# Hybrid MLA/GLA layer on one core: the MLA setup reordered on all engines, its last third moved into the first attention head

## The reference, cut to what matters

```python
cq, ckv, kr, gq, gk, gv, gr, gg = split(x @ w_in)         # 384, 256, 64, 256, 256, 512, 16, 512
# A) MLA, 4 heads of 128 + 64
q = (rms_norm(cq, q_norm) @ w_uq).reshape(B, T, 4, 192)
q_rope = apply_rope(q[..., 128:], cos, sin)
k_rope = apply_rope(kr, cos, sin)
ckv = rms_norm(ckv, kv_norm)
s = causal((q_nope . w_uk . ckv) + (q_rope . k_rope)) * MLA_SCALE
mla = softmax(s) @ ckv @ w_uv
# B) GLA, 4 heads, chunks of 64 tokens
loga = log_sigmoid(gr @ w_gate2 + b_gate) / 16
S_t = diag(exp(loga_t)) S_(t-1) + k_t^T v_t;  o_t = q_t S_t
gla = rms_norm(o, gla_norm) * silu(gg)
x = layer_norm(ALPHA * x + concat(mla, gla) @ w_out)
y = layer_norm(ALPHA * x + square(relu(x @ w1)) @ w2)     # 4096 wide
```

## Time and profile before

| what | value |
|---|---|
| median of 3 runs | 1426.96 us (1426.54 to 1427.34) |
| the profiled execution | 1429.95 us |
| its span | 1428.3 us |
| mean granted clock of TensorE | 0.97 |
| PE busy | 1344.7 us, 94% of the span, 8796 instructions |
| PEld busy | 1260.5 us, 88% |
| DVE busy | 605.7 us, 42%, 950 instructions |
| ACT busy | 414.4 us, 29% |
| POOL busy | 158.8 us, 11% |
| DMA | 123.38 MB, mean 86 GB/s |

### The profile page before, as it was taken

One profiled execution on the slowest core, in us unless ns is written; L12 is line 12 of the kernel. 1 busy time (PEld: TensorE's weight loads), 2 busy tenths in 40 slices (PEclk: granted clock), 3 DMA queues, 4 the chain that ended last, 5 costly groups with the idle time before them and its releaser, 6 DMA issues.

```text
span 1428.3 us, 22125 instructions
## 1 busy us (share of the span) xinstructions
PE 1344.7 (94%) x8796; PEld 1260.5 (88%) x8796; DVE 605.7 (42%) x950; ACT 414.4 (29%) x677; POOL 158.8 (11%) x195
## 2 busy tenths in 40 slices
PE   7998999999878897999999999999999999999996
PEld 7986868787657776899999999999999999999996
DVE  4122222445776776565532422314233133242558
ACT  3212332234534445534411302203022031120225
POOL 4424333010000000042000000000000000004022
PEclk9999999999879998999999999999999999999998
DMA  8658886413300011312120301102012020020103
GB/s 285 206 181 266 281 281 217 119 60 95 107 17 10 10 45 60 104 46 59 58 62 1 95 24 59 59 0 88 29 39 79 0 88 29 29 88 0 59 1 119
DMA packets 100593, 123.38 MB, mean 86 GB/s; under 512 B 11123, under 2 KB 84997, under 8 KB 100518
## 3 DMA queue, kind: packets, MB, share of 16 engines
q1 hardware_dynamic: 94374, 105.59, 23.5%
q0 software_dynamic: 6144, 16.79, 3.7%
HBM read 108.42 MB, written 13.93 MB: 86 GB/s over the span
## 4 chain that ended last, share of the span: by engine, by line
PE 80%; SPq 7%; DVE 7%; issue 3%; ACT 2%; DMA 1%; POOL 0%; DVEq 0%; ACTq 0%; POOLq 0%
PE psum L2120 24%; PE psum L2148 22%; PE psum L355 9%; PE psum L1843 6%; PE psum L1353 5%; SPq L267 3%; SPq L270 3%; PE psum L2087 3%; PE psum L1664 2%; PE psum L2081 2%; DVE softmax_stats L1735 1%; PE psum L904 1%; PE psum L901 1%; DVE pT_lo L1753 1%; PE psum L1673 1%
## 5 line engine op out<-in xcount | busy, mean ns | idle before, releaser
L2177 ACT ACTIVATE hid_tmp<-psum 128x1032 f32<-128x1032 f32 x32 | 33.1, 1035 | 531.0 <-PE psum L2120 526.4
L355 PE MATMUL psum<-xTh,win_hi 128*128 128x344 f32 (+1 forms) x432 | 150.5, 348 | 9.7 <-DVE xTl L408 9.7
L2120 PE MATMUL psum<-x_hi,w_hi 128*128 128x344 f32 x720 | 153.2, 321 | 0.0
L2120 PE MATMUL psum<-x_lo,w_hi 128*128 128x344 f32 x720 | 152.8, 320 | 0.0
L2120 PE MATMUL psum<-x_hi,w_lo 128*128 128x344 f32 x720 | 152.0, 319 | 0.0
L2148 PE MATMUL psum<-hid_hi,w_hi 128*128 128x344 f32 x672 | 142.6, 320 | 0.0
L2148 PE MATMUL psum<-hid_lo,w_hi 128*128 128x344 f32 x672 | 142.4, 320 | 0.0
L2148 PE MATMUL psum<-hid_hi,w_lo 128*128 128x344 f32 x672 | 141.8, 319 | 0.0
L355 PE MATMUL psum<-xTl,win_hi 128*128 128x344 f32 (+1 forms) x432 | 141.5, 328 | 0.0
L355 PE MATMUL psum<-xTh,win_lo 128*128 128x344 f32 (+1 forms) x432 | 141.5, 328 | 0.0
L2242 DVE TENSOR_TENSOR z_T<-z_T,psum 128x1032 f32<-128x1032 f32 x48 | 59.0, 1229 | 186.7 <-PE psum L2148 186.7
(11 more groups left out here) (387 smaller groups left out, 2182.1 us busy)
## 6 DMA issues: line engine op xcount, KB each, us to landing
mlp_raw<-in_w SPq DMA_DIRECT2D x64, 512.0 KB, 4.3
k_pages<-in_pages SPq DMA_DIRECT2D x128, 160.0 KB, 3.2
v_pages<-in_pages POOLq DMA_DIRECT2D x128, 128.0 KB, 4.2
win_raw<-in_w_in SPq DMA_DIRECT2D x17, 512.0 KB, 6.6
scratch<-proj_stage SPq DMA_DIRECT2D x13, 516.0 KB, 5.1
x_T_raw<-in_x_T SPq DMA_DIRECT2D x6, 688.0 KB, 9.2
z_T<-in_x_T SPq DMA_DIRECT2D x3, 1376.0 KB, 6.2
out_y_T<-z_T SPq DMA_DIRECT2D x12, 344.0 KB, 2.4
```

The source lines that it names most:

```text
L355: mm = pe.matmul(psum[0:M, 3 * (m % 2) + b, 0:BLK], w[:, m % 2, k, 0:M], x[:, k, b * BLK:(b + 1) * BLK], start=(k == 0 and i == 0), stop=( ...
L2120: mm = pe.matmul(psum[:, 3 * (i % 2) + b, 0:BLK], w[:, i % 2, k], x[:, k, C3[b]], start=(k == 0 and n == 0), stop=(k == KD - 1 and n == 2))
L2177: act.activation(ht[:, i % 2, :].rearrange("p (b c) -> p b c", b=3), mlp_set(i), ACT.Relu).then_inc(h_free, 1)
```

## The change

It touches the order of the work, not its amount: no product is added or left out.

1. **Gate loads.** In `sp_project` the call of `sp_gates_in` moves from ahead of tile 6's work to behind the issue of tile 6's store.
2. **State stores.** The four stores of the sample's GLA state leave `sp_gla` for `sp_gla_sample`, which is called ahead of `sp_heads_in`, so that they stand ahead of the load of cq.
3. **Rotary tables** get buffers of their own (in the room of the even key's high and low part) and are loaded behind the key rows, with no wait for "nk". The second pair gets its own input and temporary (`xr2`, `rtmp2`).
4. **Query sums.** The squares and their additions move up into GLA's slots 46 to 50 (`act_cq_squares`, `dve_cq_sum`), with rows of `mixT` as their place (`sqrow`); "nq" moves to the end of the "gla_bank" ring, behind gT0 to gT3. Head weights and rotary weights are split in slots 46 to 50.
5. **Head 0's query and key blocks** are done within the setup (`QK_FIRST`), right behind pair 0's swaps. "head_bank" now continues the counts of "gla_bank".
6. **Into the first head** (table `EXTRA`, by unit v): pair 1's swaps (0), eight value blocks (2 to 5), gT4 to gT7 and gTs (3 to 5), GLA's second root, normalisation and sample (`dve_gla_normed`, 2); the even key's split and pair 1's low part (1). Head 1's query blocks go from units 2 and 4 to units 5 and 6.

The table and the functions that run it:

```diff
@@ sp_project @@
-                if m == ROW_KR + 1:
-                    sp_gates_in(sp)
...
                 sp.dma_start(scratch[m, 0:rows, :], pstage[0:rows, m % 2, :]).then_inc(proj_stored[m % 2], 16)
+                if m == ROW_KR + 1:
+                    sp_gates_in(sp)
                 after(3 * m + 2)
...
@@ ring of banks 6 and 7 in GLA and setup @@
-                   44: [("sO",)], 47: [("nk",)], 50: [("gT", 0), ("gT", 1)], 53: [("gT", t) for t in range(2, 5)]}
+                   44: [("sO",)], 47: [("nk",)]}
         SLOTS = 12 * (NT - ROW_GG)
-        gb = Banks("gla_bank", [6, 7], [task for s in range(SLOTS + 6) for task in gla_tasks(s)] + [("gT", t) for t in range(5, 8)] + [("gTs",)])
+        GLA_LAST = [("gT", 0), ("gT", 1), ("gT", 2), ("gT", 3), ("nq",)]
...
@@ sp_gla @@
+        def sp_gla_sample(sp):
             sp.wait_ge(st_done, 4)
...
@@ ScalarE, slots 46, 48 and after @@
+        def act_cq_squares(act, k):
+            if k == 0:
+                act.wait_ge(cq_loaded, 16)
+                act.wait_ge(cksq_done, 3)
+            elif k == 1:
+                gb.wait(act, ("nk",))
+            else:
+                act.wait_ge(cqsum_done, 1)
+            act.activation(sqrow[0 if k else 1], cqraw[:, k], ACT.Square).then_inc(cqsq_done, 1)
...
@@ VectorE, slots 49 and after @@
+        def dve_cq_sum(dve, k):
+            dve.wait_ge(cqsq_done, k + 1)
+            dve.tensor_tensor(sqrow[1], sqrow[1], sqrow[0], ALU.add).then_inc(cqsum_done, 1)
...
@@ SyncE, rotary tables @@
-            gb.wait(sp, ("nk",))
-            r = a["rope"].rearrange("p (c t) -> p c t", c=2)
-            for i in range(2):
-                sp.dma_start(rope[i], r[:, i, 0:TP]).then_inc(rope_loaded, 16)
...
+            r = a["rope"].rearrange("p (c t) -> p c t", c=2)
+            for i in range(2):
+                sp.dma_start(rope[i][:], r[:, i, 0:TP]).then_inc(rope_loaded, 16)
...
@@ pe_mla_in @@
-            split(pe, "cq2")
-            pe_rope_in(pe, 0)
-            for t in range(NORM_A, 8):
+            pe_rope_in(pe, 0, 1)
+            for t in (1, 2, 3):
                 pe_gla_task(pe, ("gT", t))
-            pe_gla_task(pe, ("gTs",))
-            pe_rope_swap(pe, 0)
-            pe_rope_in(pe, 1)
-            mb.begin(pe, ("nq",))
-            pe.wait_ge(cqsum_done, 2)
-            mb.full(pe_norm_sums(pe, mb.of(("nq",)), cqsq[:, 0]))
-            pe_rope_swap(pe, 1)
-            split(pe, "uv")
-            for t in range(8):
-                mb.begin(pe, ("v", t))
-                c = slice(t * P, (t + 1) * P)
-                mb.full(passes(pe, mb.of(("v", t)), [((ckh[:, k, c], ckl[:, k, c]), (wuvh[:, k], wuvl[:, k])) for k in range(2)]))
+            pe_gla_task(pe, ("nq",))
+            pe_rope_swap(pe, 0, mb)
+            pe_qk(pe, ("q", 0, 0)), pe_qk(pe, ("q", 0, 1))
+            pe_rope_in(pe, 1, 0)
+            split(pe, "ck1")
+            pe_qk(pe, ("k", 0, 0)), pe_qk(pe, ("k", 0, 1))
+            pe_rope_in(pe, 1, 1)
 
...
@@ dve_mla_in, behind the key's low parts @@
-            lo_of(dve, "kr0")
+            gated(dve, 2)
+            variance(dve, 1)
+            gated(dve, 3)
+            dve_var_rms(dve, 1, ("nq",), 3 * P)
             dve.wait_ge(gst_stored, 80)
-            lo_of(dve, "kr1"), lo_of(dve, "uv")
-            dve_rope(dve, 0)
+            lo_of(dve, "kr1")
+            dve_qk(dve, ("q", 0, 0)), dve_qk(dve, ("q", 0, 1))
+            dve_rope(dve, 0, mb)
-            dve_var_rms(dve, 1, mb, ("nq",), 3 * P)
-            dve_rope(dve, 1)
-            lo_of(dve, "q1")
+            dve_qk(dve, ("k", 0, 0)), dve_qk(dve, ("k", 0, 1))
-            for t in range(8):
-                lo_of(dve, f"v{t}")
-            head_lo(dve, 0)
-
...
@@ the table, and the ring of the heads @@
+        EXTRA = {0: [("qs", 1, 0), ("qs", 1, 1)], 2: [("v", 0), ("v", 1), ("v", 2)], 3: [("v", 3), ("gT", 4), ("gT", 5)],
+                 4: [("gTs",), ("v", 4), ("v", 5), ("gT", 6)], 5: [("gT", 7), ("v", 6), ("v", 7)]}
+        QK_FIRST = [("q", 0, 0), ("q", 0, 1), ("k", 0, 0), ("k", 0, 1)]
...
+            at = (5, 6) if h == 1 else (2, 4)
+            return [("q", h, at.index(i))] if i in at else [("k", h, b) for b in range(2)] if i == 7 else []
...
+        W_TASKS = list(QK_FIRST)
         for v in range(UNITS + 3):
...
+            W_TASKS += EXTRA.get(v, []) + qk_tasks(v)
+        wk = Banks("head_bank", [6, 7], W_TASKS, gb)
         tp = Banks("pT_bank", [4, 5], [(u, g) for u in range(UNITS) for g in range(1 + (u % 8 >= 4))])
...
+        def pe_extra(pe, v):
+            for key in EXTRA.get(v, ()):
+                if key[0] == "v":
+                    t = key[1]
+                    c = slice(t * P, (t + 1) * P)
+                    if t == 0:
+                        split(pe, "uv")
+                    wk.begin(pe, key)
+                    wk.full(passes(pe, wk.of(key), [((ckh[:, k, c], ckl[:, k, c]), (wuvh[:, k], wuvl[:, k])) for k in range(2)]))
+                elif key == ("qs", 1, 0):
+                    pe_rope_swap(pe, 1, wk)
+                elif key[0][0] == "g":
+                    pe_gla_task(pe, key, wk)
+
+        def act_extra(act, v):
+            for key in EXTRA.get(v, ()):
+                if key[0] == "v":
+                    wk.wait(act, key)
+                    if key[1] == 0:
+                        split(act, "kr0")
+                    act.activation(vh[:, key[1]], wk.of(key), ACT.Copy).then_inc(wk_hi, 1)
+                elif key == ("qs", 1, 1):
+                    act.wait_ge(qrope_done, 2)
+                    hi_of(act, "q1")
+            if v == 1:
+                hi_of(act, "kr0")
+
+        def dve_extra(dve, v):
+            for key in EXTRA.get(v, ()):
+                if key[0] == "v":
+                    t = key[1]
+                    dve.wait_ge(wk_hi, HI.index(key) + 1)
+                    wk.free(dve.tensor_tensor(vl[:, t], wk.of(key), vh[:, t].bitcast(F32), ALU.subtract), key)
+                elif key[0] == "gT":
+                    gated(dve, key[1], wk)
+                elif key == ("gTs",):
+                    gated_sample(dve, wk)
+                elif key == ("qs", 1, 0):
+                    dve_rope(dve, 1, wk)
+            if v == 1:
+                lo_of(dve, "q1"), lo_of(dve, "kr0")
+            if v == 2:
+                dve_gla_normed(dve)
```

More of the change, by code:

```diff
@@ L863, in pe_slot, with pe_gla_task @@
                     pe_gla_task(pe, task)
-        def pe_gla_task(pe, key):
+        def pe_gla_task(pe, key, bank=None):
+            bank = bank or gb
             name, t = key[0], key[-1]
@@ L871, in pe_gla_task @@
                 pe.wait_ge(lg_done, 2)
-            gb.begin(pe, key)
-            o = gb.of(key)
+            bank.begin(pe, key)
+            o = bank.of(key)
             if name == "cum":
@@ L944, in pe_gla_task @@
                     mm = pe.transpose(o[:, i * P:(i + 1) * P], os_[:, i, :], ident)
-            gb.full(mm)
+            bank.full(mm)
         def pe_gla(pe):
@@ L1190, in normed, with gated @@
                 ins.then_inc(gon_done, 1)
-        def gated(dve, t):
+        def gated(dve, t, bank=None):
+            bank = bank or gb
             key = ("gT", t)
             c = slice(t * P, (t + 1) * P)
-            gb.wait(dve, key)
+            bank.wait(dve, key)
             if t == 0:
@@ L1414, in pe_norm_sums, with pe_rope_in, pe_rope_swap @@
             return mm
-        def pe_rope_in(pe, pr):
-            for b in range(2):
-                mb.begin(pe, ("qr", pr, b))
-                mb.full(passes(pe, mb.of(("qr", pr, b)), [((wrh[:, pr, k], wrl[:, pr, k]), (cqh[:, k, C2[b]], cql[:, k, C2[b]])) for k in range(3)]))
-        def pe_rope_swap(pe, pr):
-            for b in range(2):
-                mb.begin(pe, ("qs", pr, b))
+        def pe_rope_in(pe, pr, b):
+            key = ("qr", pr, b)
+            mb.begin(pe, key)
+            for k in range(3):
+                if pr == 0 and b == 0:
+                    split(pe, f"cq{k}")
+                mm = passes(pe, mb.of(key), [((wrh[:, pr, k], wrl[:, pr, k]), (cqh[:, k, C2[b]], cql[:, k, C2[b]]))], start=(k == 0), stop=(k == 2))
+            mb.full(mm)
+        def pe_rope_swap(pe, pr, bank):
+            for b in range(2):
+                key = ("qs", pr, b)
+                bank.begin(pe, key)
                 pe.wait_ge(qx_done, 2 * pr + b + 1)
-                mb.full(pe.matmul(mb.of(("qs", pr, b)), const("swap"), xr[:, pr, C2[b]], start=True, stop=True))
+                bank.full(pe.matmul(bank.of(key), const("swap"), xr[pr][:, C2[b]], start=True, stop=True))
         def pe_mla_in(pe):
             pe.wait_ge(proj_out, NT)
+            pe_gla_task(pe, ("gT", 0))
+            pe_rope_in(pe, 0, 0)
             pe.wait_ge(rk_done, 1)
@@ L1501, in head_lo, with dve_var_rms @@
             dve.tensor_tensor(wql[:], wqraw[:], wqh[:].bitcast(F32), ALU.subtract).then_inc(wh_lo, 1)
-        def dve_var_rms(dve, i, bank, key, n):
```

(15 more changed lines are left out.)

240 lines of the change are left out of this document (111 added, 129 removed).

## The result

The changed kernel takes 1431.34 us (median of 12 runs, 1426.27 to 1433.74), the kernel before 1427.70 (12 runs, 1424.58 to 1433.82): a ratio of 1.0026, 95% interval 1.0014 to 1.0037, so 2 to 5 us slower. The profiled execution took 1431.47 with a span of 1429.8.

What follows compares the result with a forecast made beforehand. It took TensorE's waits for late key pages behind SyncE's list and its idle gaps in the MLA setup as the bounds to work on. -3.9 + 0.45 = -3.45 us against a median of 1426.96 gave 1423.5 us, range 1415.0 to 1429.5.

Steps and rivals of the forecast that it cites:

- Part 1: Page loads on SyncE: gate loads behind tile 6's store remove 3.9 us between tile 5's store and them, -3.9 us.
- Rival B: Page loads gain nothing because the DMA engines are full; 1427.4 us, same as before, chance 0.15.
- Part 2: MLA setup from the last state update to the first scores: scores 0 start 29.3 us earlier, at 404.6.
- The new wait: TensorE in the setup stops 5.8 us before the query sums, until a gated block on VectorE frees their bank.
- Part 3: First head takes in the moved work: 28.2 of 29.3 us come back at full clock; net taken as +0.45.
- the middle: Setup and first head together: +0.45 us, taken between -1.1 at the full clock and +2.0 at the low one.
- the dearer case: First head at the low clock: v2, transpose 5 and scores 4 take 3.1 us more, +2.0 instead of -1.1.
- The sum: Whole kernel: -3.9 for the page loads and +0.45 for setup and first head, -3.45 us, giving 1423.5 us.
- A: First head: VectorE packs better, hand-overs overlap more, floor 14.6 us lower, half kept; 1416 us, chance 0.22.
- C: First head: holes put TensorE at the low clock repeatedly, slower, 1431.0 us; decides above 33.2 us given back; chance 0.13.

Runs made afterwards that it cites:

- e1: The kernel before with only the gate loads moved behind tile 6's store; 1425.32 us, ratio 0.9983 to the kernel before.
- e2: The changed kernel with the gate loads put back ahead of tile 6's work; 1435.20 us, ratio 1.0052 to the kernel before.
- e7: The changed kernel with the key norm's two broadcasts ahead of the first half's rotary products; 1430.72 us, ratio 1.0033 to the kernel before.
- e3: The changed kernel with six unread 512-column products in TensorE's gap ahead of the query sums; 1426.73 us, ratio 0.9999 to the kernel before.

## Why the prediction was wrong

**Part 1** (forecast -3.9): right in its mechanism, its size known only to lie between -2.2 and -3.9, the two pairs of medians; the load behind the store moved by 3.95, of which 2.2 was left once the gate loads had had their turn. Rival B, which gave part 1 nothing, is made unlikely by e1 and e2 together and by the places of the state update.

**Part 2** (forecast: scores 0 29.3 us earlier; measured 24.5) is the step that failed. Its timetable was close in what it named: the sums, computed at the low clock, take 3.57 against 3.54. The new wait before them, computed as 5.8, is 5.80, but that is luck: both of its ends came 3.4 us late. Counted from its own state update (367.5) the timetable has scores 0 after 37.1 us; they came after 42.46, so 5.4 late. (That is 4.8 against the kernel before, as the timetable had the state update itself 0.5 later, which the traces can't show.) Two of its assumptions gave this away.
- "From there VectorE's list has no hole." It has one of 2.62 before the scaling of ckv, which waits for TensorE's broadcasts, and the sums start 21.6 us after the state update instead of 18.2. I had TensorE through its rotary products and transposes 12.4 us after the state update (379.9 - 367.5); it took 15.8, and e7 showed that TensorE's list, not the order within it, was the limit. The list was late because of the clock, which is at 0.50 from 362.2 to 371.0, 8.8 us behind the state update. In the kernel before it had risen some 2.5 us behind it, as the same products show, first before, then changed:

```profile
371.17 0.49 PE L901 MATMUL psum<-gv,a_masked 128*128 128x128 f32 x2
```

```profile
366.38 0.80 PE L905 MATMUL psum<-gv,a_masked 128*128 128x128 f32 x2
```

  Some 6 us more at half the clock are worth up to 3 us, an estimate that covers most of the 3.4. All twelve kernels with the new setup have the clock low for 7 to 10 us there; why it lasts longer than before, no run isolates.
- "The swaps end at 391.2, then two query blocks, 2.2 each." I put only the sums at the low clock. The swaps took 3.76 and the first query product 1.42, and scores 0 lost 2.0 more. A row of my own list should have warned me: swaps of 3.75 behind a wait of 5.64, the size of the new wait. e3 measured all that the clock costs behind this wait, sums included, at 3.7 us.

**Part 3** (forecast: 28.2 us come back at the full clock, 31.3 at the low one; measured 29.6): the size was right, the places too (holes of 2.2 and 3.3 us forecast before v2 and gT5, 3.54 and 3.34 measured). I took the middle for lack of a reason to choose, so that the 29.6 falls on it is partly luck: the clock was low behind the first hole (0.50 from 420.0 to 425.6), full behind the second, where the dearer case had it low (1.00 from 431 to 445), and low behind scores 0, where I had it full.

**The sum**: -3.9 + 0.45 forecast, -2.2 to -3.9 and +5.1 measured; of the 4.7 between the second terms nearly all is part 2. What the parts give, +1.2 to +2.9, lies at and under the lower end of the measured 2 to 5. The rest isn't placed: behind row block 7 the profiled executions take 970.4 and 970.5 us with the old lists (before, e1) and 969.2 to 972.0, on average 0.8 more, in the twelve with the new ones, and a spread of 2.8 tells nothing.

**The rivals.** A (better packing of VectorE) has nothing for it: VectorE is busy 37.2 of 53.5 us in the first head. C had the sign, the mechanism (the clock at its low level behind waits) and by chance the time, 1431.0, but it put the loss into the first head and had it decide at 33.2 us given back; 29.6 were, and what the forecast missed lay ahead of scores 0. The Trainium skill (TensorE: Matmul & The Clock Gate, HAM oscillation) describes a kernel in which each burst of products behind a wait starts at the low clock. For this setup the trace agrees, sums and swaps at 0.50 behind 5.80 us of waiting, and e3, which fills the wait, has them at 1.00; behind the 3.34 us before gT5 it does not, the clock stays at 1.00. I gave that rule 13% and should have applied it to the setup as well.

## What to carry to other kernels

When a change puts a wait in front of a chain of work, price the chain behind it at the low clock until a row shows otherwise, not the first instruction alone. A small task at the end of a ring of two banks inherits the waits of every task ahead of it; moving it two places up, and its reader with it, was worth 8.4 us here, the clock's 3.7 included. And where work is moved into a later stage, count first who is full there: the head took 29.6 us for 24.5 won, until the work on VectorE that fitted an earlier gap (2.2 us) and the values that fitted a gap of TensorE (2.5 us) went into these.
